# Splitting a 31-tap convolution over three engines, with a wider norm, a gate projection per group and one projection stage moved

## The reference, cut to what matters

```python
u = rms_norm_3(h, ln_g[i]);  z = u @ w_in[i]            # [1024, 7168]
c_val, c_glu, c_gate, hq, hf, hi, hg = split(z, 7)       # 1024 columns each
v = c_val * sigmoid(c_glu)
y = causal_depthwise_conv(v, conv_w, taps=31) + conv_b   # per channel, over time
y = silu(group_layer_norm(y, cn_g, cn_b, n_groups=8))    # 8 groups of 128 channels
y = y @ w_pw2 + b_pw2;  y_conv = y * silu(c_gate)        # done in a later stage
# hgrn2_branch(hq, hf, hi, hg): 8 recurrent heads of 128 channels
```

## Time and profile before

| | |
|---|---|
| median of three runs | 4603.8 us |
| the profiled execution, its own time | 4599.1 us |
| its span | 4597.1 us, 48973 instructions |
| TensorE busy | 3863.9 us (84%) |
| VectorE busy | 2217.1 us (48%) |
| ScalarE busy | 1700.9 us (37%) |
| GpSimd busy | 532.2 us (12%) |
| the convolution stage | 3056.8 to 3468.4 us of the span |
| projections of the first recurrent head | 3468.4 to 3517.4 us |

### The profile page before, as it was taken

The page is one execution under the profiler, slowest core; times in us unless marked ns, Lnnn a source line. Parts: engine busy times, 40 slices in busy tenths (PEclk is TensorE's granted clock), DMA queues, the critical chain, the costliest instruction groups (busy, mean ns, idle before and its releaser), DMA issues.

```text
span 4597.1 us, 48973 instructions
## 1 busy us (share of the span) xinstructions
PE 3863.9 (84%) x20470; PEld 3187.3 (69%) x20470; DVE 2217.1 (48%) x2728; ACT 1700.9 (37%) x2231; POOL 532.2 (12%) x450
## 2 busy tenths in 40 slices
PE   5978589999986897788888877957868999959988
PEld 5866587787864676666666647945656878748988
DVE  3233334343346565444554442279993565653222
ACT  3322131211113555455565651124445454521122
POOL 0000000100002334200000000020002232320002
PEclk9977799999997998899999988978988999979999
DMA  2221311111101001101000004111111111123111
GB/s 81 69 88 37 124 56 50 46 46 46 46 29 65 28 28 37 37 21 35 23 24 23 26 13 158 38 55 55 54 52 42 33 37 33 37 86 116 47 35 63
DMA packets 196848, 232.30 MB, mean 51 GB/s; under 512 B 8391, under 2 KB 168084, under 8 KB 196628
## 3 DMA queue, kind: packets, MB, share of 16 engines
q1 hardware_dynamic: 190868, 208.20, 13.8%
q10 hardware_dynamic: 5760, 20.97, 1.2%
HBM read 185.10 MB, written 44.04 MB: 50 GB/s over the span
## 4 chain that ended last, share of the span: by engine, by line
PE 57%; DVE 20%; ACT 10%; issue 8%; DMA 2%; POOL 2%; SPq 0%; ACTq 0%; DVEq 0%; POOLq 0%
PE pd L211 49%; PE pq L211 6%; DVE t L2447 6%; ACT t L2173 2%; DVE t L2225 2%; DVE t L321 2%; PE pd L355 2%; ACT t L312 1%; DVE t L1327 1%; PE pq L355 1%; DVE t L511 1%; DMA t<-ym_scratch 0%; DVE t L1637 0%; DVE t L540 0%; DVE t L2243 0%
## 5 line engine op out<-in xcount | busy, mean ns | idle before, releaser
L211 PE MATMUL pd<-t 128*128 128x512 f32 (+2 forms) x15920 | 3126.8, 357 | 139.2 <-DVE t L582 54.5
L211 PEld LDWEIGHTS pd<-t 128*128 128x128 f32 x15920 | 2583.9, 193 | 634.6 <-issue 189.2
L211 PE MATMUL pq<-t 128*128 128x128 f32 (+5 forms) x3222 | 619.4, 365 | 257.5 <-ACT t L2477 49.5
L211 PEld LDWEIGHTS pq<-t 128*128 128x128 f32 (+2 forms) x3222 | 424.4, 202 | 398.3 <-issue 79.5
L312 ACT ACTIVATE t<-t 128x2048 fp32r<-128x2048 f32 (+2 forms) x130 | 240.4, 1849 | 723.2 <-PE pd L211 694.1
L321 DVE TENSOR_TENSOR t<-t 128x2048 fp32r<-128x2048 f32 (+2 forms) x130 | 303.7, 2336 | 344.5 <-ACT t L312 344.5
L355 PE MATMUL pd<-t 128*128 128x128 f32 x960 | 160.8, 321 | 207.9 <-DVE t L485 59.8
L2447 DVE SCALAR_TENSOR_TENSOR t<-t 128x1024 f32<-128x1024 f32 x240 | 307.7, 1284 | 11.9 <-ACT t L2437 5.4
L355 PEld LDWEIGHTS pd<-t 128*128 128x128 f32 x960 | 136.0, 168 | 237.5 <-issue 67.3
L1278 DVE TENSOR_TENSOR t<-pd,t 128x512 f32<-128x512 f32 x256 | 172.1, 689 | 128.0 <-PE pd L211 128.0
L2173 ACT ACTIVATE t<-t 128x1024 f32<-128x1024 f32 x128 | 146.2, 1144 | 94.2 <-DVE t L2230 94.1
(11 more groups left out here) (268 smaller groups left out, 2838.8 us busy)
## 6 DMA issues: line engine op xcount, KB each, us to landing
t<-in_w_in_dram SPq DMA_DIRECT2D x89, 512.0 KB, 5.1
t<-in_w_mlp_dram SPq DMA_DIRECT2D x32, 1024.0 KB, 5.4
t<-in_w_in_dram SPq DMA_DIRECT2D x20, 1024.0 KB, 5.2
t<-in_w_out_dram SPq DMA_DIRECT2D x20, 1024.0 KB, 5.2
t<-ym_scratch ACTq DMA_DIRECT2D x24, 512.0 KB, 8.6
ym_scratch<-t SPq DMA_DIRECT2D x20, 512.0 KB, 2.6
t<-in_x_dram SPq DMA_DIRECT2D x16, 512.0 KB, 5.1
gs_scratch<-t SPq DMA_DIRECT2D x16, 512.0 KB, 2.7
```

Of the source, the lines that this page charges most:

```text
L211: ins = e.matmul(out, l, r, start=(first and j == 0), stop=(last and j == n - 1), skip_group_check=True)
```

## The change

- Taps 0 to 9 of each group are made by ScalarE, each as a product into a tile of a ring of three (`Tap`), and added up by GpSimd with nine 128x1024 `tensor_tensor` (`Sum3`). VectorE starts its accumulator with tap 10 as a `tensor_scalar`, adds taps 11 to 30 and then GpSimd's sum: 22 instructions for 30.
- The tail works on 1024 columns at a time where it worked on 512 twice (TensorE's matmuls stay 512 wide).
- The gate projection is one unit of 128 columns and two `fm` in each group.
- The first recurrent head's eight `fm` and their activations are woven with the last group and the last tail; the fence lies behind them. The recurrent setup moves to the start of the convolution stage; the masks lie side by side and are converted at its end.
- The ring `Sg3` has five tiles for six, and memory is laid out so that the first head's buffers don't lie over the convolution's.

In the diff `AT_` is 10, `both` gives the two `pq` halves as one operand, `rec0` is the generator of the first recurrent head's projections, and the calls that count semaphores (`.then_inc(...)`) are left off.

```diff
-    def act_conv_light(e, g):
-        a = e.take(Acc3, "cacc", g)
-        e.activation(a[:, :], p[:, 0:S], ACT.Identity, scale=taps(0, g), bias=pc("cb3", g))
+    def act_conv_light(e, g):
+        e.wait_ge(*at["cin", g, 1])
+        for k in range(AT_):
+            m = e.take(Tap, "ctap", g, k)
+            if k == 0:
+                e.activation(m[:, :], p[:, 0:S], ACT.Identity, scale=taps(0, g), bias=pc("cb3", g))
+            else:
+                e.mul(m[:, :], p[:, k:k + S], taps(k, g))
+            yield from idle(3)
+    def pool_conv_light(e, g):
+        c = e.take(Sum3, "csum", g)
+        e.tensor_tensor(c[:, :], Tap.of("ctap", g, 0)[:, :], Tap.of("ctap", g, 1)[:, :], ADD)
+        for k in range(2, AT_):
+            e.wait_ge(*at["ctap", g, k])
+            e.wait_ge(*at["csum", g, k - 1])
+            e.tensor_tensor(c[:, :], c[:, :], Tap.of("ctap", g, k)[:, :], ADD)
     def dve_conv_light(e, g):
-        e.wait_ge(*at["ctap0", g])
-        for k in range(1, 31):
+        e.tensor_scalar(a[:, :], p[:, AT_:AT_ + S], taps(AT_, g), None, MUL)
+        yield
+        for k in range(AT_ + 1, 31):
             e.scalar_tensor_tensor(a[:, :], p[:, k:k + S], taps(k, g), a[:, :], MUL, ADD)
             yield
+        e.wait_ge(*at["csum", g, AT_ - 1])
+        e.scalar_tensor_tensor(a[:, :], Sum3.of("csum", g)[:, :], 1.0, a[:, :], MUL, ADD)
...
     def dve_conv_tail(e, g):
-        for th in range(2):
-            e.tensor_tensor(a[:, sl], a[:, sl], PB.of("cmu", g, th), SUB)
-            e.tensor_tensor(a[:, sl], a[:, sl], sg[:, sl], MUL)
+        e.wait_ge(*at["cmu", g])
+        e.tensor_tensor(a[:, :], a[:, :], both("cmu", g), SUB)
+        yield from idle(4)
+        e.wait_ge(*at["crs", g])
+        e.scalar_tensor_tensor(a[:, :], a[:, :], 1.0, sg[:, :], MUL, MUL)
...
-    def pe_gate3(e, n):
-        u = pe_unit(e, W3in, [(2048 + n * 256, 256)])
+    def pe_conv_side(e, g):
+        if g < 7:
+            yield from pe_conv_dense(e, g + 1)
+        if g >= 0:
+            u = pe_unit(e, W3in, [(2048 + g * 128, 128)])
...
-        steps(dense(e, 0))
-        for g in range(8):
-            parts = [(light(e, g), 31), (side(g), 7 if g % 2 else 4)]
-            if g > 0:
-                parts.append((tail(e, g - 1), 14))
-            weave(*parts)
-        steps(tail(e, 7))
+    def conv_stage(e, light, n, side, tail, rec0):
+        steps(side(e, -1))
+        r = rec0(e, 0)
+        for g in range(8):
+            s_ = side(e, g)
+            parts = [(light(e, g), n), (chain(s_, islice(r, 4)) if g == 7 else s_, 6)]
+            if g > 0:
+                parts.append((tail(e, g - 1), 9))
+            weave(*parts)
+        weave((tail(e, 7), 9), (r, 6))
...
     def rec_stage(e, who, dense, rec, out_):
-        steps(dense(e, 0))
```

More of the change, by code:

```diff
@@ L2380, in program, with both @@
     ph = ExitStack()
[L2381 to L2385, removed]
+    M128 = sbt(ph, [128, S])
+    lb, lb1 = sbt(ph, [128, 8]), sbt(ph, [128, 8])
+    Mi = sbt(ph, [128, 8, 128], I32)
+    Mf = sbt(ph, [128, 7, 128])
+    At = sbt(ph, [128, NT, 128])
+    vT = sbt(ph, [128, S])
+    Sr = ring(ph, 2, [128, 128])
+    dec3 = sbt(ph, [128, 8])
+    RB = [[sbt(ph, [128, S]) for _ in range(4)] + [sbt(ph, [128, NT, 128])]]
+    ph2 = ExitStack()
+    Pad = ring(ph2, 2, [128, S + 30])
+    Acc3 = ring(ph2, 2, [128, S])
+    Tap = ring(ph2, 3, [128, S])
+    Sum3 = ring(ph2, 2, [128, S])
+    Sg3 = ring(ph2, 5, [128, S])
+    c128 = sbt(ph2, [128, 128])
+    eps3 = sbt(ph2, [128, 1])
+    ph2.close()
+    ph2 = ExitStack()
+    RB.append([sbt(ph2, [128, S]) for _ in range(4)] + [sbt(ph2, [128, NT, 128])])
+    Dr_ = ring(ph2, 3, [128, S])
+    Zr = ring(ph2, 3, [128, S])
+    kdt3 = sbt(ph2, [128, NT, 128])
+    O3 = sbt(ph2, [128, NT, 128])
+    ph2.close()
     ph.close()
+    LV = [64, 32, 16, 8, 4, 2, 1]
+    AT_ = 10
     def taps(k, g):
         return pc("cw3a", 8 * k + g) if k < 16 else pc("cw3b", 8 * (k - 16) + g)
-    def pool_conv(e):
-        for i, p in enumerate(Pad.tiles):
-            e.memset(p[:, 0:30], 0.0).then_inc(*at.inc("pool", "pad3", i))
+    def both(*key):
+        i = PB.place.get((*key, 0), 0)
+        assert i % 2 == 0
+        return PQt[i // 2][:, :]
     def dve_conv_setup(e):
@@ L2406, in pe_conv_dense @@
         pe_done(u)
-    def act_conv_dense(e, g):
-        act_unit(e)
-        sg = e.take(Sg3, "cglu", g, hold=True)
-        for th in range(2):
-            e.wait_ge(*at["cglu", g, th])
-            e.activation(sg[:, half(th)], PD.of("cglu", g, th)[:, :], ACT.Sigmoid).then_inc(
-                *at.inc("act", "csig", g, th, free=("cglu", g, th)))
+    def pe_conv_side(e, g):
[3 more added lines that the diff above has]
+            u = pe_unit(e, W3in, [(2048 + g * 128, 128)])
+            for th in range(2):
+                fm(e, u, 0, th, 3, "cz", g, th)
+                yield
+            pe_done(u)
@@ new lines, in act_conv_side @@
+    def act_conv_side(e, g):
+        if g < 7:
+            act_unit(e)
+            sg = e.take(Sg3, "cglu", g + 1)
+            for th in range(2):
+                yield
+                e.wait_ge(*at["cglu", g + 1, th])
+                e.activation(sg[:, half(th)], PD.of("cglu", g + 1, th)[:, :], ACT.Sigmoid).then_inc(
+                    *at.inc("act", "csig", g + 1, th, free=("cglu", g + 1, th)))
+                yield
+        if g >= 0:
+            act_unit(e)
+            sg = e.take(Sg3, "cz", g)
+            for th in range(2):
+                yield
+                e.wait_ge(*at["cz", g, th])
+                e.activation(sg[:, half(th)], PD.of("cz", g, th)[:, :], ACT.Silu).then_inc(
+                    *at.inc("act", "czs", g, th, free=("cz", g, th)))
@@ new lines, in dve_conv_side @@
+    def dve_conv_side(e, g):
+        if g < 7:
+            dve_unit(e)
+            p = e.take(Pad, "cpad", g + 1)
+            yield
+            for th in range(2):
+                yield
+                e.wait_ge(*at["csig", g + 1, th])
+                e.wait_ge(*at["cval", g + 1, th])
+                e.wait_ge(*at["pad3", 1])
+                e.tensor_tensor(p[:, 30 + th * 512:30 + th * 512 + 512], PD.of("cval", g + 1, th)[:, :],
+                                Sg3.of("cglu", g + 1)[:, half(th)], MUL).then_inc(
+                    *at.inc("dve", "cin", g + 1, th, free=("cval", g + 1, th)))
+                yield
+            at.also("dve", ("cglu", g + 1))
+        if g >= 0:
+            dve_unit(e)
+            yield
+        if g == 7:
@@ L2415, in act_conv_dense, with sp_conv_side @@
             yield
             yield
[L2417 to L2422, removed]
-            yield
[L2424 to L2429, removed]
-            yield
-        at.also("dve", ("cglu", g))
+    def sp_conv_side(e, g):
+        if g < 7:
+            sp_unit(e)
+            yield
+            yield
+        if g > 0:
+            sp_gate3(e, g - 1)
+        yield
+        yield
+        if g >= 0:
+            sp_unit(e)
+            yield
@@ L2433, in act_conv_light, with sp_gate3 @@
+    def sp_gate3(e, g):
+        e.wait_ge(*at["czs", g, 1])
+        e.dma(ZG[g * 128:(g + 1) * 128, :], Sg3.of("cz", g)[:, :], "zg3", g, free=("cz", g))
     def act_conv_light(e, g):
-        a = e.take(Acc3, "cacc", g)
         p = Pad.of("cpad", g)
         e.wait_ge(*at["cin", g, 1])
-        e.activation(a[:, :], p[:, 0:S], ACT.Identity, scale=taps(0, g), bias=pc("cb3", g)).then_inc(
-            *at.inc("act", "ctap0", g))
-        yield from idle(30)
-    def dve_conv_light(e, g):
-        a, p = Acc3.of("cacc", g), Pad.of("cpad", g)
-        e.wait_ge(*at["ctap0", g])
-        for k in range(1, 31):
-            if k > 1:
-                e.wait_ge(*at["ctaps", g])
+        for k in range(AT_):
+            m = e.take(Tap, "ctap", g, k)
+            if k == 0:
+                e.activation(m[:, :], p[:, 0:S], ACT.Identity, scale=taps(0, g), bias=pc("cb3", g)).then_inc(
+                    *at.inc("act", "ctap", g, 0))
+            else:
+                e.mul(m[:, :], p[:, k:k + S], taps(k, g)).then_inc(*at.inc("act", "ctap", g, k))
+            yield from idle(3)
+        at.also("act", ("cpad", g))
@@ new lines, in pool_conv_light @@
+    def pool_conv_light(e, g):
+        c = e.take(Sum3, "csum", g)
+        e.wait_ge(*at["ctap", g, 0])
+        e.wait_ge(*at["ctap", g, 1])
+        e.tensor_tensor(c[:, :], Tap.of("ctap", g, 0)[:, :], Tap.of("ctap", g, 1)[:, :], ADD).then_inc(
+            *at.inc("pool", "csum", g, 1, free=("ctap", g, 0)))
+        at.also("pool", ("ctap", g, 1))
+        for k in range(2, AT_):
+            e.wait_ge(*at["ctap", g, k])
+            e.wait_ge(*at["csum", g, k - 1])
+            e.tensor_tensor(c[:, :], c[:, :], Tap.of("ctap", g, k)[:, :], ADD).then_inc(
+                *at.inc("pool", "csum", g, k, free=("ctap", g, k)))
@@ L2447, in dve_conv_light @@
+    def dve_conv_light(e, g):
+        p = Pad.of("cpad", g)
+        a = e.take(Acc3, "cacc", g)
```

(83 more changed lines are left out.)

40 lines of the change are left out of this document (17 added, 23 removed).

## The result

| | before | after |
|---|---|---|
| median | 4603.99 us (6 runs, 4600.86 to 4605.29) | 4620.62 us (6 runs, 4618.15 to 4622.69) |
| the profiled execution, its span | 4597.1 us | 4618.7 us |

The changed kernel is 16.6 us slower; the ratio is 1.0037, with a 95% interval from 1.0024 to 1.005.

The account below looks back on a forecast made before the run. VectorE, mostly its taps, was taken to bound the convolution's middle. Middle 52 us longer, start 1.3 earlier, end 34.7 shorter: 16 us slower, 4615 from the profiled execution, 4620 as median; range 4588 to 4645.

Parts of the forecast that it names:

- VectorE's own work in the middle: Middle of the convolution stage: VectorE's instructions after the change, counted at uncontended durations, come to 277.3 us.
- an addition's price on VectorE: Convolution middle: each of 72 GpSimd additions blocks VectorE for 2.0 us; less 4 us overlap, 140 us in all.
- middle: Middle of the convolution stage: 277.3 + 140 = 417 us against 365.2, 52 us longer.
- VectorE waits for the last sum: Each convolution group: GpSimd's last addition ends at 41 us, VectorE's sum comes at 52; slack 11 us, no wait.
- end, to the head's first instruction: From VectorE's last instruction of the convolution to the first recurrent head: 35 us against 69.7, 34.7 us less.
- sum: Whole kernel: 52 - 1.3 - 34.7 = 16 us slower, forecast 4620 us.
- The bound from below: Lowest price per addition on VectorE, 0.67 us of a 512-wide addition x 2 = 1.34 us.
- The walk through one group: One convolution group in queue order: subtraction at 10 to 12 us, product about 33, last addition ended at 41.
- The sum of the end: Convolution's end: chain through mean, products, variance, last product's copy ahead of Ln, Silu, store and fence; 35 us taken.
- The share of VectorE's work that can run beside an addition: Convolution middle: input products and subtractions with one PSUM input, 18.1 us or 6.5%; 4 us taken off.
- The rival without exclusion: Convolution middle: taps and additions don't exclude each other, TensorE bounds at 39 us per group; 89 us faster, 4515; chance 0.14.
- The statement that nothing else waits: One convolution group walked in queue order: no wait besides the turns VectorE takes with GpSimd's additions.

## Why the prediction was right

| step | forecast | measured |
|---|---|---|
| VectorE's own work in the middle | 277.3 us | about 275.9 (the new forms at their measured 0.75, 1.22 and 1.23) |
| an addition's price on VectorE | 2.0 us, 4 off in all: 1.94 net | 1.96 ((417.1 - 275.9)/72); 1.93 and 2.03 by the steps to five and two taps |
| middle | 417 us | 417.1 us |
| start of the middle | 1.3 us earlier | 0.9 (1.15 us behind the input product for 2.01) |
| VectorE waits for the last sum | no, 11 us of slack | no, 10.2 us of slack in most groups, 5.2 in the last |
| end, to the head's first instruction | 35 us | 35.5 us |
| sum | 16 us slower, 4620 | 16.8 us by the steps above; medians 16.6 apart, 4620.62 |

The step that carried it is the price per addition. Its source is one pair of lines of the same form and size as the new additions, one of 14 alike, and a second pair that showed the taps' own operation in the same turn-taking. The bound from below, 1.34 us, would have given 32 us faster, so the choice of 2.0 carried the sign. The walk through one group came out too: in the fourth group (start 3242.2) the subtraction stands at 10.3 us (10 to 12), the product at 34.6 (33) and the end of the last addition at 41.0 (41). The sum of the end named the right order, down to the copy that holds Ln, which the run with the earlier tail shows to be that. The gain on the end and the loss in the middle were each twice or three times the net, so the sign hung on both being right to about 15 us.

That the total came within 1 us is partly luck. The share of VectorE's work that can run beside an addition was put at 6.5%, which would be 9 us of the 144; the sum took 4 off and gave no reason, and 4 fits. In the end two errors cancel: the last product ended 23.0 us behind the last sum for 25, and from the last Silu to the head it took 4.1 us for 2.8. The anchor was no luck: the profiled execution of before, 4599.1 us, is 4.9 below its median and that of the changed kernel, 4620.45, is at its own, so the pair differs by 21.4 us; 16.8 of them are the steps above, and the rest stands in front of the stage (1.0) and behind the head's start (3.6). The forecast went from median to median, which differ by 16.6.

Smaller steps were off. The rival without exclusion was priced at 39 us per group for TensorE, 4515; with an accumulator that needs no second SBUF input the kernel runs at 4508.8, with 38.5 us per group, and with memsets for additions at 36.7. The sum and the product, which have an immediate scalar, take 1.23 and 1.22 us, where I took the tap's 1.284; that the scalar is the reason is not shown. The statement that nothing else waits holds, but the time that additions take is not only on taps: VectorE's instructions in the middle are 144 us longer than alone, of which 127 are on taps (332.2 - 160 x 1.284), 15 on weight halves, 2 on the norm's product.

## What to carry to other kernels

Before work is moved from VectorE to GpSimd, look for an instruction of VectorE with two SBUF inputs beside a GpSimd instruction that reads SBUF: if both durations are longer than alone, with no idle time, most of the moved work's duration on GpSimd comes back on VectorE, here 1.94 of 2.34 us, in place of a tap of 1.284. Moving fewer taps helps (27 us for five), but the better cure here is other operands: with the accumulator in PSUM the same split of ten taps gained 112 us. And a projection stage can hide behind a tail that leaves TensorE idle (31 us here), if the tail's chain comes first in the queues of the engines that both share (9 us).

## What I had not expected of the hardware

- A `tensor_scalar` of 128x1024 takes 0.75 us into SBUF, and 1.288 us into PSUM; a tap takes 1.285 us with its accumulator in SBUF and 1.290 in PSUM (medians). Rows of the changed kernel and of the one with the accumulator in PSUM:

```profile
L2535 DVE TENSOR_SCALAR t<-t x8: 747/748/753, 3082.8 to 3450.8; 128x1024 f32<-128x1024 f32 x8
L2537 DVE TENSOR_SCALAR pq<-t 128x1024 f32<-128x1024 f32 x8 | 10.3, 1288 | 0.7 <-DVE t L2475 0.5
```

- The granted clock of TensorE (0.50 is 1.2 GHz, 1.00 is 2.4 GHz; here means over a middle) was the lower, the longer TensorE had stood: 0.87 in the changed kernel, where it was idle for 13.7 us of each group, 0.90 before with 11.0, 0.98 with seven taps and 2.2, and 1.00 with memsets and 0.25. So a faster VectorE gave TensorE a part of its time back too: 291.7 us of busy time for the products that took 307.4.
